# Moving activation tiles by multiples of 32 bytes in SBUF in a two-block transformer kernel on one core

## What is computed

```python
# first block
hx = modulate(rmsnorm(x, g_norm1), mx[0], mx[1])
px = split(hx @ w_in, IN_SPLIT_IDX)          # attention and gated recurrence
x = x + mx[2] * (concatenate([att_x, hg_x]) @ w_out)
a, b = split(modulate(rmsnorm(x, g_norm2), mx[3], mx[4]) @ w_gu, 2)
x = x + mx[5] * ((silu(a) * b) @ w_down)     # D_FF = 2816
# second block
proj = rms_norm(x, g_pre_mix) @ w_in_2       # qa ka va latents gates
merged = gates[:, :D] * (o_a @ w_branch_a) + gates[:, D:] * (o_b @ w_branch_b)
x = x + rms_norm(merged @ w_out_2, g_post_mix)
m = square(relu(rms_norm(x, g_pre_mlp) @ w_up)) @ w_down_2   # D_FF_2 = 4096
x = x + rms_norm(m, g_post_mlp)
```

## Time and profile before

| | |
|---|---|
| median of 3 runs | 816.3 us (815.54 to 817.55) |
| the profiled execution | 816.35 us, of which the span is 814.6 us |
| TensorE busy | 788.6 us, 97% of the span |
| weight loads busy | 693.1 us, 85% |
| VectorE, ScalarE, GpSimd busy | 429.5, 418.7, 376.7 us |
| granted TensorE clock, mean | 0.997 |
| DMA | 146.61 MB, 180 GB/s on average |

### The profile page before, as it was taken

One profiled execution on the slowest core, in us unless ns is written; L12 is line 12 of the kernel. 1 busy time (PEld: TensorE's weight loads), 2 busy tenths in 40 slices (PEclk: granted clock), 3 DMA queues, 4 the chain that ended last, 5 costly groups with the idle time before them and its releaser, 6 DMA issues.

```text
span 814.6 us, 14292 instructions
## 1 busy us (share of the span) xinstructions
PE 788.6 (97%) x5493; PEld 693.1 (85%) x5493; DVE 429.5 (53%) x684; ACT 418.7 (51%) x641; POOL 376.7 (46%) x181
## 2 busy tenths in 40 slices
PE   6999999999899999999999999999999999999996
PEld 4778877887777999999997889999897999999995
DVE  4675568984667533332336747645355343423435
ACT  5335426454846444544444955654766645444443
POOL 3126000000164654566545986565455554666452
PEclk9999999999999999999999999999999999999998
DMA  9984567134953666556654787433455556656641
GB/s 319 308 277 132 177 225 267 53 105 104 331 185 107 201 189 203 182 180 182 201 167 129 228 208 189 131 105 131 145 167 171 163 182 191 195 186 191 190 154 52
DMA packets 94396, 146.61 MB, mean 180 GB/s; under 512 B 15741, under 2 KB 64110, under 8 KB 94352
## 3 DMA queue, kind: packets, MB, share of 16 engines
q1 hardware_dynamic: 92896, 143.23, 56.1%
q0 software_dynamic: 1424, 2.77, 1.2%
q10 hardware_dynamic: 32, 0.01, 0.0%
HBM read 144.93 MB, written 1.06 MB: 179 GB/s over the span
## 4 chain that ended last, share of the span: by engine, by line
PE 81%; DVE 8%; issue 3%; DMA 3%; ACT 2%; POOL 2%; SPq 0%; DVEq 0%; ACTq 0%; POOLq 0%
PE bank L1881 78%; POOL w_lo L632 2%; ACT w_hi L697 1%; PE bank L2151 1%; DVE hg_at L1436 1%; DVE w_lo L1200 1%; PE bank L1972 1%; DVE hg_queries L1387 1%; DMA raw<-in_w_in 1%; DMA raw<-in_w_mod 1%; DMA gate_mlp_b<-gate_rows 1%; DMA x<-in_x 1%; PE bank L2459 1%; DVE x L1833 1%; DVE stat L1517 1%
## 5 line engine op out<-in xcount | busy, mean ns | idle before, releaser
L632 POOL TENSOR_TENSOR w_lo<-raw,w_hi 128x1024 fp32r<-128x1024 f32 (+2 forms) x150 | 361.6, 2427 | 312.7 <-ACT w_hi L697 310.8
L697 ACT ACTIVATE w_hi<-raw 128x1024 fp32r<-128x1024 f32 (+1 forms) x218 | 226.3, 1046 | 210.2 <-PE bank L1881 185.5
L1200 DVE TENSOR_TENSOR w_lo<-raw,w_hi 128x1024 fp32r<-128x1024 f32 x71 | 87.9, 1248 | 136.2 <-ACT w_hi L697 136.1
L1881 PE MATMUL bank<-z_hi,w_hi 128*128 128x256 f32 x384 | 109.1, 284 | 0.1
L1881 PE MATMUL bank<-z_hi,w_lo 128*128 128x256 f32 x384 | 107.6, 280 | 0.0
L1881 PE MATMUL bank<-z_lo,w_hi 128*128 128x256 f32 x384 | 107.5, 280 | 0.0
L1881 PE MATMUL bank<-n_hi,w_hi 128*128 128x256 f32 x352 | 99.3, 282 | 1.1 <-POOL w_lo L632 1.1
L1881 PE MATMUL bank<-n_hi,w_lo 128*128 128x256 f32 x352 | 98.9, 281 | 0.0
L1881 PE MATMUL bank<-n_lo,w_hi 128*128 128x256 f32 x352 | 98.9, 281 | 0.0
L1881 PE MATMUL bank<-w_hi,mlp_h_hi 128*128 128x512 f32 x216 | 84.2, 390 | 0.0
L1881 PE MATMUL bank<-w_lo,mlp_h_hi 128*128 128x512 f32 x216 | 84.1, 389 | 0.0
(11 more groups left out here) (419 smaller groups left out, 1593.0 us busy)
## 6 DMA issues: line engine op xcount, KB each, us to landing
raw<-in_w_in SPq DMA_DIRECT2D x54, 512.0 KB, 4.7
raw<-in_w_down SPq DMA_DIRECT2D x54, 512.0 KB, 4.1
raw<-in_w_gu SPq DMA_DIRECT2D x44, 512.0 KB, 3.6
raw<-in_w_up SPq DMA_DIRECT2D x32, 512.0 KB, 3.8
raw<-in_w_mod SPq DMA_DIRECT2D x24, 512.0 KB, 4.0
raw<-in_w_mod SPq DMA_DIRECT2D x32, 256.0 KB, 6.1
raw<-in_w_out SPq DMA_DIRECT2D x12, 512.0 KB, 4.1
raw<-in_w_in SPq DMA_DIRECT2D x8, 336.0 KB, 3.0
```

Of the source, the lines that this page charges most:

```text
L632: nc.gpsimd.tensor_tensor(wl[:, w % SPL, 0:size], raw[:, slot_raw, 0:size], wh[:, w % SPL, 0:size].bitcast(F32), ALU.subtract).then_inc(s_ ...
L697: nc.scalar.activation(wh[:, w % SPL, 0:size], raw[:, slot_raw, 0:size], ACT.Copy).then_inc(s_hi, 1)
L1200: V.tensor_tensor(wl[:, w % SPL, :], raw[:, slot_raw, :], wh[:, w % SPL, :].bitcast(F32), ALU.subtract).then_inc(s_lod, 1)
L1881: return nc.tensor.matmul(out_, l, r_, start=start, stop=stop, skip_group_check=True)
```

## The change

Six `apart` tiles are added or resized. Everything behind them moves; nothing else is edited. In bytes a float counts four, so `[P, 24]` is 96 bytes per partition.

```diff
@@ first block, the MLP's tiles @@
         hm = sb("mlp_h", [P, 2, 512], F32, r)
+        sb("apart_h", [P, 56], F32, r)
         mh = sb("mlp_h_hi", [P, 2, 512], F32R, r)
@@ first block, ahead of n @@
         sb("region2", [P, 4096], F32, b1)
-        sb("apart_n", [P, 48], F32, b1)
+        sb("apart_n", [P, 24], F32, b1)
...
@@ second block @@
         yn = sb("yn", [P, 2, D], F32, b2)
-        sb("apart_z", [P, 48], F32, b2)
+        sb("apart_z", [P, 8], F32, b2)
         zh = sb("z_hi", [P, KT, T], F32R, b2)
         zl = sb("z_lo", [P, KT, T], F32R, b2)
-        sb("apart_zf", [P, 80], F32, b2)
+        sb("apart_zf", [P, 120], F32, b2)
         zf = sb("z_f32", [P, 4, T], F32, b2)
         gates = sb("gates", [P, 16, T], F32, b2)
+        sb("apart_o", [P, 16], F32, b2)
         oh = sb("o_hi", [P, 8, T], F32R, b2)
         ol = sb("o_lo", [P, 8, T], F32R, b2)
+        sb("apart_m", [P, 112], F32, b2)
...
         h2 = sb("mlp2_h", [P, 3, 512], F32, r)
+        sb("apart_h2", [P, 8], F32, r)
         h2h = sb("mlp2_h_hi", [P, 3, 512], F32R, r)
```

## The result

The changed kernel takes 822.5 us (median of 4 runs, 821.79 to 823.32), the kernel before 816.36 us on the same chip: ratio 1.0073, 95% interval 1.0061 to 1.0086. It is slower by 6 us.

A forecast was written before the change was run, and what follows sets the result against it. TensorE was taken as the bound, through the spacing of matmul starts. The terms 2.2 + 1.4 + 1.9 - 0.3 - 0.4 = +4.8 us on 816.3 us gave 821.1 us; range for 8 in 10, 803.5 to 830 us.

The forecast's parts named there:

- o, 0 to 64: Streamed o matmuls, 192 of them: spacing goes from 120.0 to 117.9 ns, -0.4 us.
- n at 96: Streamed n matmuls of the first MLP, 1056 of them: spacing rises to 120.0 ns, +2.2 us.
- The reason given: For streamed n and z: 192 already shows the lower pace, and an odd multiple of 32 is no nearer 192 than 0.
- z at 32: Streamed z matmuls: spacing rises to 120.0 ns, +1.4 us in the second MLP's loop, +1.9 us in gates and head.
- The split h "I leave it at 226.5: 0 us": Stationary split h in both MLPs, 648 matmuls with 512 weight columns streamed: spacing stays at 226.5 ns, 0 us.
- z as the stationary operand: z held stationary while 512 weight columns stream, 144 matmuls: 2.2 ns a step less, -0.3 us.
- The bound of 237 ns: Worst spacing allowed for the stationary split h matmuls, about 237 ns; the best was 217 ns.
- The sum: All parts of the whole kernel together: 2.2 + 1.4 + 1.9 - 0.3 - 0.4 = +4.8 us, giving 821.1 us.
- F: Odd distances keep weight load and stream apart; n and z loops at 113.5 ns, -12.4 us, 803.9 us; chance 0.36.
- Rival R: Only o moves, or mirrored distances make the two MLP loops cancel: 815.9 us or within 2.4 us; chance 0.18.
- L: Starts off a multiple of 64 cost some 5 ns on all 2208 + 648 matmuls: +14 us, 830 us; chance 0.10.
- The prediction's own doubt: A stage's starting pace may be set by something other than distance, such as the wait ahead of it; no size given.

The follow-up runs named there:

- experiment 9: Kernel before with the split h at distances 192 (first MLP) and 128 (second), o at 64, n and z still at 192: 813.2 us, ratio 0.9972.
- experiment 10: Kernel before with the split h at distances 192 (first MLP) and 64 (second), o at 64, n and z still at 192: 814.31 us, ratio 0.9981.
- experiment 11: Kernel before with the split h at distances 96 (first MLP) and 160 (second), o at 64, n and z still at 192: 813.4 us, ratio 0.9968.
- experiment 12: Kernel before with the split h at distances 160 (first MLP) and 96 (second), o at 64, n and z still at 192: 813.69 us, ratio 0.9975.
- experiment 2: Kernel before with only n and z moved, to distances 96 and 32 as in the change: 819.0 us, ratio 1.0037.
- experiment 4: Kernel before with the mirrored distances: n 32, z 96, split h 32 (first MLP) and 224 (second), o 160: 822.8 us, ratio 1.0085.
- experiment 7: Kernel before with only the split h moved, to distances 192 (first MLP) and 128 (second): 811.76 us, ratio 0.9954.
- experiment 1: Kernel before with only the split h moved as in the change, to distances 224 (first MLP) and 32 (second): 816.93 us, ratio 1.0016.
- experiment 5: Kernel before with only the split h moved, to distances 32 (first MLP) and 224 (second): 815.75 us, ratio 1.0001.
- experiment 3: Kernel before with an unused 32-byte tile ahead of w_hi, moving weights and everything behind them, distances unchanged: 816.96 us, ratio 1.0016.
- experiment 6: Kernel before with only the split h moved, to distances 64 (first MLP) and 192 (second): 814.08 us, ratio 0.9979.
- experiment 8: Kernel before with no tile moved, one 2-column matmul added ahead of each up run in the second MLP's loop: 819.71 us, ratio 1.0048.

## Why the prediction was right, and where it was not

The forecast was 821.1 us and slower; 822.5 was measured, ratio 1.0073. By its own steps:

1. **o, 0 to 64**: forecast -0.4 us at 117.9 ns, measured 117.8 ns and -0.4. Right for this execution; in experiments 9 to 12 the same distance shows 113.3 ns as well.
2. **n at 96**: forecast 120.0 ns and +2.2 us, measured 120.0 and +2.4. Right in size. The reason given, that an odd multiple of 32 is like distance 0, is not: z at 32 shows 116.7.
3. **z at 32**: forecast +1.4 in the loop and +1.9 elsewhere, measured -0.7 and +0.7. This step failed. It took one value for both odd distances; experiments 2 and 4 show that 32 and 96 differ by 3.3 ns and that the value goes with the distance, not with the stage.
4. **The split h "I leave it at 226.5: 0 us"**: the term that was mis-sized. Measured 233.3 ns, +4.2 us, the largest of all, and +0.6 for z as the stationary operand, where -0.3 was forecast. The two rows at hand, 226.5 at 0 and 228.7 at 192, were read as the middle of the range; the other distances (232.4 to 234.2 at 32, 64, 96, 128, 160 and 224) show that they are its two best cases. The bound of 237 ns had allowed for it.
5. **The sum**: steps 3 and 4 erred by -3.3 and +5.1 us (4.2 + 0.6 + 0.3) and in part cancelled. That the total came within 1.4 us is luck. The sign owes less to it: without the split h the parts come to +2.6 us, and experiment 2, in which only n and z move, is slower by 3.2.

Of the rivals, F had a true core that the change itself destroyed: a pace of 113.5 ns in the loops can be had, with n and z left at 192 and the split h moved (both loops in experiments 7, 9, 11 and 12, one in 1, 5 and 10). Rival R has two halves. Its mirror had something: n at 96 lost 2.3 ns and z at 32 gained 1.1 in the loops, opposite in sign, but not alike in size, and the split h lost on both sides. That nothing moves, R's other half and the rule of the two ports, falls with experiments 1, 2 and 4; the two read ports that the Trainium skill gives TensorE ("SBUF — State Buffer", section "SBUF: two separate sides") do not make the distance harmless here. L falls with experiment 3. The prediction's own doubt, that the pace with which a stage starts may be set by something other than the distance, was the right one: experiments 1 and 5 show that the run ahead has a part in it, and the branches of experiment 9 show the pace changing at a wait.

What stays open. That the weight load and the streamed operand hinder each other in SBUF is argued from the distance being what counts and from both reading at once; no run took the weight load away. All experiments move activation tiles against everything else, so a distance to some other tile, one that another engine writes at the same time, is not excluded by a run of its own; against it stands that z and the split h, two tiles in different stages, have the same spacing as stationary operands at the same distance from the weights (z 229.0 and h 229.0 to 229.7 at 192, both near 233.3 at 32, 234.2 and 233.9 at 96). What a `down` run hands on is not known, nor what decides the pace behind a wait. Since 192 keeps the pace that it finds, and that pace was 113.3 ns in some executions and 117.8 in others, a kernel with the split h at 192 should have two times. Experiment 6 fits: its profiled execution, with z at the long pace, was the slowest of its ten at 816.74 us; less 672 x 4.3 ns = 2.9 us that is 813.9 us, an estimate, and the median was 814.08. No second profile of the same kernel was taken to show it.

## What to carry to other kernels

When TensorE is busy without a gap, take the spacing of successive starts for each pair of operands; if equal shapes have different spacings, look at the distance of the two operands in SBUF before anything else, since an unused tile of some bytes was worth 2 to 6 ns a matmul here. Judge such a shift by the spacing in every stage, the next one included, and try each tile by itself: a layout that lengthens one run by 6 ns a step can still win by the pace that it leaves to the run behind it. Where a stage has two paces, one profile shows one of them; look at the spread of the times as well. A value that lies between two bounds need not be typical; the rows at hand may all come from layouts that had been picked.

## What the runs showed of the hardware

- For fp32r matmuls with 128 stationary columns, the mean spacing by the distance of the activation tile from the weights, modulo 256 bytes. Activations stationary, 512 columns of weights streamed: 226.8 ns at 0 in the MLPs (227 to 228 in the other stages), 229.0 to 229.7 at 192, 232.4 to 234.2 at the other multiples of 32. Activations streamed, 256 columns: 119.8 at 0, 120.0 at 96, 116.7 at 32 in the loops (116.5 to 118.0 in short runs elsewhere), 118.3 at 160 (one stage of one kernel), 113.3 or 117.8 at 64 and at 192.
- Moving all operands together by 32 bytes changed no spacing of the loops.
- Two steady paces, near 113.5 and 117.8 ns, for the same matmuls at the same addresses and a granted clock of 1.00, held over whole runs of 96 matmuls. The run of 512-column matmuls in between kept the pace, changed it or exchanged it, by the distance of its own stationary tile (the table behind experiment 12). At the first `up` runs, with no such run ahead, either pace occurred in different executions (n 117.8 ns before, 113.3 in experiment 8, ahead of the first `down` run). A 2-column matmul between the runs did not change the choice where the `down` run was at 0.
